# Mixing stage of a hybrid decoder block: gate product between a tile's two halves, branches combined first, half the weight splits behind tile 0

## What is computed

```python
z = rms_norm(h, norm_attn_g[i]) @ w_in[i]
y_attn = dilated_attention(q, k, v, rel_bias)        # three branches, weighted by their softmax denominators
y_sgu = spatial_gating(z[..., o_g:o_s], ...)         # gelu, group LayerNorm, causal 128x128 mixing, gate
y_ssm = s5_ssm(z[..., o_s:], ...)
mix = jnp.concatenate([rms_scale(y_attn), rms_scale(y_sgu), rms_scale(y_ssm)], axis=-1) * branch_norm_g[i]
h = h + mix @ w_out[i]
h = h + conv_ffn(rms_norm(h, norm_ffn_g[i]), ...)
gate = jax.nn.sigmoid(rms_norm(h, norm_ple_g[i]) @ ple_w_gate[i])
h = h + gate * (p[i] @ ple_w_proj[i])
```

## Time and profile before

| | |
|---|---|
| median of 3 runs | 2807.55 us (2801.3 to 2808.03) |
| the profiled execution | 2808.83 us, of which 2807.2 us are the span of the trace |
| PE busy | 2597.0 us, 93% of the span |
| DVE busy | 1730.9 us, 62% |
| ACT busy | 1369.6 us, 49% |
| POOL busy | 530.8 us, 19% |
| mean granted clock of PE | 0.967 of 2.4 GHz |

### The profile page before, as it was taken

One profiled execution on the slowest core, in us unless ns is written; L12 is line 12 of the kernel. 1 busy time (PEld: TensorE's weight loads), 2 busy tenths in 40 slices (PEclk: granted clock), 3 DMA queues, 4 the chain that ended last, 5 costly groups with the idle time before them and its releaser, 6 DMA issues. The chain is left out here.

```text
span 2807.2 us, 38988 instructions
## 1 busy us (share of the span) xinstructions
PE 2597.0 (93%) x13883; PEld 2232.7 (80%) x13883; DVE 1730.9 (62%) x3350; ACT 1369.6 (49%) x2459; POOL 530.8 (19%) x320
## 2 busy tenths in 40 slices
PE   6999996999964799599999999999999999997998
PEld 5889986999954688488888778888888878885876
DVE  2113195777765776678888755588888864444333
ACT  3343432666633676545555445455555543334544
POOL 3453553766510121200000000000000000000000
PEclk9999998999986899899999999999999999998999
DMA  4665555888443255122222367642222247753211
GB/s 162 190 217 164 163 165 146 186 183 184 109 135 144 94 168 193 47 83 83 75 91 85 114 233 250 226 128 75 91 87 72 90 154 247 272 174 109 77 75 47
DMA packets 313911, 392.11 MB, mean 140 GB/s; under 512 B 22161, under 2 KB 222161, under 8 KB 310650
## 3 DMA queue, kind: packets, MB, share of 16 engines
q1 hardware_dynamic: 299850, 341.60, 39.9%
q0 software_dynamic: 13888, 48.25, 4.4%
HBM read 298.59 MB, written 95.33 MB: 140 GB/s over the span
## 5 line engine op out<-in xcount | busy, mean ns | idle before, releaser
L2446 PE MATMUL ffn_bank<-ffn_x,ffn_ring 128*128 128x512 f32 x704 | 276.5, 393 | 10.8 <-DVE ffn_ring L2238 6.1
L2448 PE MATMUL ffn_bank<-ffn_x,ffn_ring 128*128 128x512 f32 x704 | 275.9, 392 | 0.0
L2447 PE MATMUL ffn_bank<-ffn_x,ffn_ring 128*128 128x512 f32 x704 | 275.6, 391 | 0.0
L2446 PE MATMUL ffn_bank<-tail_shared,ffn_ring 128*128 128x512 f32 x528 | 206.7, 391 | 9.5 <-DVE ffn_ring L2238 8.0
L516 ACT ACTIVATE att_exps<-att_scores,att_part 128x256 f32<-128x256 f32 (+1 forms) x384 | 153.1, 454 | 123.9 <-DVE att_part L487 123.6
L2448 PE MATMUL ffn_bank<-tail_shared,ffn_ring 128*128 128x512 f32 x528 | 206.2, 391 | 0.0
L1042 POOL TENSOR_TENSOR in_w_lo<-in_w,in_w_hi 128x2048 fp32r<-128x2048 f32 x36 | 168.0, 4667 | 182.5 <-ACT in_w_hi L919 182.5
L2278 DVE SCALAR_TENSOR_TENSOR ffn_strips<-ffn_strips,ffn_taps 128x512 f32<-128x512 f32 x176 | 131.9, 750 | 113.9 <-ACT ffn_strips L2082 113.9
L2513 POOL DMA_DIRECT2D ffn_act<-ffn_late x88 | 47.6, 541 | 808.7 <-DVE ffn_late L2291 808.7
L487 DVE CUSTOM_DVE_ANT_0 att_scores<-att_bank,att_bias 128x256 f32<-128x256 f32 (+1 forms) x384 | 122.5, 363 | 101.9 <-PE att_bank L434 66.2
L1012 PE MATMUL in_bank<-in_w_hi,in_hi 128*128 128x256 f32 x640 | 183.8, 287 | 0.7 <-issue 0.7
(11 more groups left out here) (347 smaller groups left out, 7194.0 us busy)
## 6 DMA issues: line engine op xcount, KB each, us to landing
ffn_w<-in_ffn_w_up SPq DMA_DIRECT2D x88, 512.0 KB, 4.7
ffn_w<-in_ffn_w_down SPq DMA_DIRECT2D x40, 1024.0 KB, 7.0
in_w<-in_w_in SPq DMA_DIRECT2D x36, 1024.0 KB, 6.3
ffn_act<-ffn_late POOLq DMA_DIRECT2D x88, 256.0 KB, 2.7
ffn_a_raw<-ffn_act SPq DMA_DIRECT2D x88, 256.0 KB, 5.6
ffn_a_raw_later<-ffn_act SPq DMA_DIRECT2D x88, 256.0 KB, 6.0
mixed_part<-branch_results SPq DMA_DIRECT2D x16, 792.0 KB, 5.4
z_rows<-in_result SPq DMA_DIRECT2D x80, 128.0 KB, 2.5
```

The source lines that it names most:

```text
L2446: pe.matmul(out[:, :], hi[:, k], x_hi[kind][:, k], start=(k == 0 and fresh), stop=False, skip_group_check=not fresh)
L2447: pe.matmul(out[:, :], hi[:, k], x_lo[kind][:, k], start=False, stop=False, skip_group_check=not fresh)
L2448: mm = pe.matmul(out[:, :], lo[:, k], x_hi[kind][:, k], start=False, stop=(k == KH - 1), skip_group_check=not fresh)
```

## The change

The order of calls changes in the lists of all engines but POOL; nothing is computed otherwise, and no instruction's size changes.

- PE: `gate_product(j+2)` goes between the two halves of tile j, behind `turn(j+1)`; before, `gate_product(j+3)` stood behind the second half. `gate_product(0, 2)` leaves the start-up.
- DVE in `step`: `finish_gate` goes from ahead of `combine` to behind `split_rows`, `add_eps` and `invert` behind it; `invert_deviation` goes directly behind `gate_statistics`.
- ACT in `step`: `root` goes behind `deviation` and `split_rows`.
- Start-up: the first tile's branches are loaded first and combined first; weight splits 4 to 7 go behind tile 0's `split_rows`.

```diff
--- before.py
+++ after.py
@@ -1387,13 +1387,13 @@
                         load_z(i, j + 3)
 
             sp.dma_start(g[:, :], gain.rearrange("(k p) -> p k", p=P), allow_slow_non_contiguous=True).then_inc(gain_loaded, DMA)
+            load_rows(0, 0)
             load_z(0, 0)
             sp.dma_start(mask_rows[:, :, :], sgu["w"].rearrange("g t s -> t g s")).then_inc(setup, DMA)
             sp.dma_start(ln_gain[:, :], sgu["ln_g"].unsqueeze(0).to_broadcast([P, GW])).then_inc(setup, DMA)
             sp.dma_start(ln_shift[:, :], sgu["ln_b"].unsqueeze(0).to_broadcast([P, GW])).then_inc(setup, DMA)
             sp.dma_start(shift_rows[:, :], sgu["b"].rearrange("g t -> t g"), allow_slow_non_contiguous=True).then_inc(setup, DMA)
             load_z(0, 1)
-            load_rows(0, 0)
             load_rows(0, 1)
             load_z(0, 2)
             load_z(0, 3)
@@ -1469,34 +1469,33 @@
                         weigh(i, j + 2)
                     if j + 3 < RING or not last:
                         gelu(i, j + 3)
-                    if j + 2 < RING or not last:
-                        root(i, j + 2)
                     if j + 3 < RING or not last:
                         deviation(i, j + 3)
                     if j + 1 < RING or not last:
                         split_rows(i, j + 1)
                     if j + 2 < RING or not last:
+                        root(i, j + 2)
                         scale_rows(i, j + 2)
                     if last and j >= 2:
                         for t in range((j - 2) * RING, (j - 1) * RING):
                             square_ahead(t)
 
             act.wait_ge(gain_loaded, DMA)
-            split_weights(0, 3)
+            split_weights(0, 2)
+            weigh(0, 0)
             for j in range(2):
                 gelu(0, j)
-            split_weights(3, 6)
+            split_weights(2, 4)
             for j in range(2):
                 deviation(0, j)
-            weigh(0, 0)
-            split_weights(6, KC)
             root(0, 0)
             scale_rows(0, 0)
             split_rows(0, 0)
+            split_weights(4, KC)
+            weigh(0, 1)
             gelu(0, 2)
+            root(0, 1)
             deviation(0, 2)
-            weigh(0, 1)
-            root(0, 1)
             scale_rows(0, 1)
             run(act, step)
 
@@ -1592,45 +1591,44 @@
                     gating = j + 3 < RING or not last
                     if more:
                         drops(i, j + 2)
-                        finish_gate(i, j + 2)
                         combine(i, j + 2)
                     if gating:
                         gate_statistics(i, j + 3)
+                        invert_deviation(i, j + 3)
                     add_resid(i, j, 0)
+                    if j + 1 < RING or not last:
+                        split_rows(i, j + 1)
                     if more:
+                        finish_gate(i, j + 2)
                         add_eps(i, j + 2)
                         invert(i, j + 2)
-                    if gating:
-                        invert_deviation(i, j + 3)
-                    if j + 1 < RING or not last:
-                        split_rows(i, j + 1)
                     add_resid(i, j, 1)
 
             dve.wait_ge(gain_loaded, DMA)
-            split_weights(0, 3)
+            drops(0, 0)
+            split_weights(0, 2)
+            combine(0, 0)
+            gate_statistics(0, 0)
+            invert_deviation(0, 0)
             dve.wait_ge(setup, 4 * DMA)
             dve.wait_ge(mask_turned, 1)
             nc.vector.tensor_copy(maskT[:, :, :], turn_bank[0].rearrange("p (g t) -> p g t", g=GROUPS)).then_inc(mask_ready, 1)
-            gate_statistics(0, 0)
-            invert_deviation(0, 0)
             gate_statistics(0, 1)
             invert_deviation(0, 1)
-            drops(0, 0)
-            split_weights(3, 5)
-            combine(0, 0)
             finish_gate(0, 0)
-            split_weights(5, 6)
+            split_weights(2, 3)
             add_eps(0, 0)
             invert(0, 0)
-            split_weights(6, KC)
+            split_weights(3, 4)
             split_rows(0, 0)
+            split_weights(4, KC)
             drops(0, 1)
-            gate_statistics(0, 2)
-            invert_deviation(0, 2)
             combine(0, 1)
             finish_gate(0, 1)
             add_eps(0, 1)
+            gate_statistics(0, 2)
             invert(0, 1)
+            invert_deviation(0, 2)
             run(dve, step)
 
         @block.tensor
@@ -1673,9 +1671,9 @@
                     products(i, j, 0)
                     if j + 1 < RING or not last:
                         turn(i, j + 1)
+                    if j + 2 < RING or not last:
+                        gate_product(i, j + 2)
                     products(i, j, 1)
-                    if j + 3 < RING or not last:
-                        gate_product(i, j + 3)
 
             pe.wait_ge(masked, GROUPS)
             for n in range(GROUPS):
@@ -1685,7 +1683,6 @@
             gate_product(0, 0)
             gate_product(0, 1)
             turn(0, 0)
-            gate_product(0, 2)
             run(pe, step)
 
         @block.gpsimd
```

## The result

| | before | after |
|---|---|---|
| median (6 runs each) | 2807.48 us | 2828.45 us (2825.62 to 2830.25) |
| ratio | | 1.0079, 95% interval 1.0066 to 1.0092 |
| profiled execution, its span | 2808.83, 2807.2 | 2829.14, 2827.5 |
| PE busy, DVE busy | 2597.0, 1730.9 | 2602.9, 1732.8 |

The account below looks back on a forecast made before the run. The DVE-ACT loop was taken to bound the kernel at 14.68 us a tile against PE's 12.69. Terms of 14.3, 2.1, 1.0 and 0.3 made +18 us; 2808.8 + 18 - 1.3 gave 2826 us, range 2815 to 2839.

Parts of the forecast that it names:

- The loop, and what bounds it: Mixing stage: DVE and ACT handing work back and forth set the pace, 14.68 us a tile against PE's 12.69; chance 0.85.
- The chain DVE-ACT: Steps and hand-overs on DVE and ACT from one invert to the next, summed to 14.68 us a tile.
- Both new waits: DVE idle each tile, about 2 us for ACT's exponential and about 1.7 us before add_eps for the squares.
- the 4.90 us of the earlier trace: PE's idle time before the gate product at 946.04 in the old kernel, which the new PE order was to remove.
- What could add to a tile: POOL's three operations running beside DVE's add_resid, split_rows and L1564: bounds 0 and 0.40 us a tile, taken as 0.
- From combine(2) to products(12,0): Loop up to the last ring: combine(2) at 932.2, combine(13) at 1093.7, products(12,0) at 1105.9, 14.3 us late.
- The end: From the last ring's start PE sets the pace again: +2.1 us for half clock, +1.0 for tile 14's gate product.
- The clock inside the loop: PE may restart at half clock after 2.0 us idle, losing up to 1.8 us a tile; costed at nothing.
- The start: Start-up with rows(0,0) loaded first: data there at 891.1, combine(2) at 932.2 instead of 935.59, 3.4 us won.
- PE stays the bound: Rival: the loop takes 12.69 us or less, so the kernel gets faster, -9 us, 2799 us; chance 0.05.
- the second rival: Loop of some 13.3 to 13.8 us, no change: +5 to +8 us, about 2814 us; chance 0.07.
- The dearer table load: Rival: ACT's Exp table load costs twice its row, loop 15.98 us, 14 us more, 2840 us; chance 0.03.

Follow-up runs that it names:

- ring-wait run: The changed kernel, but at a ring's start products(i,0) waits only for the adds up to two tiles before; 2826.68 us, ratio 1.0077.
- the exponential ahead: The changed kernel with the exponential of tile j+3 moved ahead of scale_rows(j+2) and drops(j+3) behind finish_gate(j+2); 2810.14 us, ratio 1.0020.

## Why the prediction was right

**The loop, and what bounds it: right.** The chain DVE-ACT was summed to 14.68 us. Spacing without POOL's interference is 14.73, in the changed kernel 15.05, and taking out any of three links shortens it. Both new waits came at the predicted size (2.0 and 1.7), DVE's 1.6 us for PE and the 4.90 us of the earlier trace rows are gone. One of the signs came only in part: PE was to be idle 2 us before products(j,0). It was at tiles 2 and 3 (2.2 us), 11 (1.78) and 7 (0.63), but not at tiles 5, 6, 9 and 10, where it was still catching up from the stop at the ring's start. The sum does not use this.

**The term that was mis-sized: "What could add to a tile", taken as 0 of bounds 0 and 0.40.** It measured 0.25 to 0.41 us on L1563, and 15.05 - 14.73 = 0.32 in the loop, 11 times. The overlap was called a graze, and split_rows beside POOL was taken as the nearest row; but split_rows reads PSUM, and L1549, which reads SBUF alone like L1563, was the near one. The Trainium skill (GPSIMD Engine Reference, Key points) says the same: POOL contends with DVE instructions that have two SBUF inputs. By it the sum was to be up to 4 us higher; POOL cost 3.7. The trace agrees: instructions with one PSUM input beside POOL (L1585, 0.69; L1578, 1.28 for two) took no longer.

**From combine(2) to products(12,0).** combine(2) was to start at 932.2 and did at 931.78; combine(13) was to start at 1093.7 and came at 1098.33. Of these 5 us between, about 3.7 are POOL (0.34 us on L1563 at the median, 11 times), the rest small hand-overs and the ring starts, where the spacing was 15.3. products(12,0) came 19.4 late instead of 14.3.

**The end: right within 0.5 us.** From products(12,0) to the last add it is 1161.04 - 1110.94 = 50.1 us, against 1139.01 - 1091.56 = 47.45 before: 2.65 more. Forecast were 3.1, 2.1 for the clock and 1.0 for gate product 14. The first half took 1118.23 - 1110.94 = 7.3 us instead of 5.5, so the clock cost 1.8; the gate product takes 0.8 us here, from 1119.10 to the next matmul at 1119.92. The prediction let products(1,0) begin at 948.0, the end of the gate product's row; its first matmul stands at 947.76, so that half took 7.6 us and not 7.3.

**The clock inside the loop, costed at nothing under cover of PE's idle time: right.** After 2.20 us idle at 955.62 PE went on at full clock, after 2.21 at 970.81 it was at the lower level for some us. Busy time by stretch, the 6 us behind each:

```profile
955.60:961.60 6.00, 5.99 (x28) 4.97 (x29) 2.48 (x8) 4.20 (x11) 1.32 (x2) 1.00 0.11 12
970.80:976.80 6.00, 5.99 (x19) 4.81 (x20) 2.33 (x8) 4.35 (x11) 1.28 (x2) 0.72 0.10 20
```

The slower start lengthens the tile's products and shortens PE's next idle time, as in the ring-wait run above (0.40 us at 1102.26 behind the slow tile of 1087.28, otherwise 2.2), and the spacing of the tiles stays.

**The start: right.** drops(0,0) came at 890.85 (891.1 forecast). The stage began 1.2 us earlier in this execution, though; counted from the load of `mixed_gain`, combine(2) came after 48.7 us, with 48.0 forecast and 51.4 before. What it won is small, as forecast, and only shows where the loop leaves room.

**Luck in the number.** The stage is 23.2 us longer, and the sum had 18: it was 5 us short, mostly the POOL term. The profiled executions differ by only 20.3 us and the medians by 21.0, since what lies outside the stage took 2.9 us less, which nothing in the change explains. So 2826 lies nearer to 2828.45 than the sum by itself deserved.

**The rivals.** That PE stays the bound needed the wait for the exponential gone; the exponential ahead gives 13.3 us a tile, so it would not have been enough. It also prices the second rival, a loop of 13.3 to 13.8 us: that run lies 5.6 us above its kernel before, within the +5 to +8, but only because each ring's first tile takes 14.8 us; by the prediction's own terms a loop of 13.3 us gives 2.5 (combine(13) 1.5 early, then 0.6, 2.1, 1.0 and 0.3). The link that decides is finish_gate with the squares behind it. The dearer table load is out: the exponential starts 1.29 us behind its load. The Trainium skill (ScalarE: Activation LUTs, What ACT_TABLE_LOAD costs) has 1.38 us of drain besides; no row here shows such a gap.

## What to carry to other kernels

When an order of work is changed to free the bounding engine, write down the new ring of hand-overs among the engines that had slack, and sum it over a tile: a step that two engines pass back and forth must have other work standing between its parts. Here one call placed two steps too late, finish_gate behind split_rows instead of ahead of add_resid, turned a gain of 0.2% into a loss of 0.8%. And price a wait by what is late next, not by its length.

## What was unexpected

- A VectorE instruction of 256 columns with both inputs in SBUF took 0.67 to 0.83 us beside GpSimd instead of 0.43, and each time it ended 0.28 us after GpSimd's operation. A wait added to GpSimd took 3.7 us out of the loop.
- PE idle for 2.2 us kept its clock at one tile and lost it at the next: 1.00 and 0.72 granted over the next 6 us. The idle time just before does not tell it alone: in the run with the shorter ring wait 1.00 was granted over the 6 us behind 2.20 us idle at 1072.06, and 0.72 behind 2.23 at 1087.28 and behind 2.08 at 1117.32.
- A wait of 6.07 us of PE, just ahead of the part that PE bounds, was worth 1.8 us there when it was taken away, and nothing that the medians can tell.
